# A mixture-of-experts block: the last expert's down matrix by column halves

## The reference, cut to what matters

```python
def expert(args):
    xt, w1e, w3e, w2e = args
    return (jax.nn.silu(xt @ w1e) * (xt @ w3e)) @ w2e

ye = lax.map(expert, (xe.swapaxes(0, 1), w1, w3, w2))
ye = ye.swapaxes(0, 1) * gate[..., None].astype(ye.dtype)
ye = ye.reshape(B, N_EXPERTS * cap, D)
return jax.vmap(lambda y, i: jnp.zeros((S, D), y.dtype).at[i].add(y))(
    ye, idx.reshape(B, N_EXPERTS * cap))
```

## Time and profile before

| | us |
|---|---|
| median of 3 runs | 1906.71 |
| the three runs | 1904.84, 1906.71, 1906.79 |
| span of the profiled execution | 1904.77 |
| the profiled execution's own time | not given apart from its span |
| TensorE busy (share of the span) | 1745.2 (92%) |
| VectorE busy | 550.8 (29%) |
| ScalarE busy | 224.1 (12%) |
| mean rate of the DMAs over the span | 314 GB/s |

### The profile page before, as it was taken

One profiled execution on the slowest core, in us unless ns is written; L12 is line 12 of the kernel. 1 busy time (PEld: TensorE's weight loads), 2 busy tenths in 40 slices (PEclk: granted clock), 3 DMA queues, 4 the chain that ended last, 5 costly groups with the idle time before them and its releaser, 6 DMA issues.

```text
span 1904.8 us, 20203 instructions
## 1 busy us (share of the span) xinstructions
PE 1745.2 (92%) x8202; PEld 774.4 (41%) x8202; DVE 550.8 (29%) x1479; ACT 224.1 (12%) x439; POOL 56.1 (3%) x61
## 2 busy tenths in 40 slices
PE   9999999999999999998988889898898988989888
PEld 8544575544465433332333323333333333323332
DVE  2343373496552322211212022121221112211111
ACT  2331151002471200000000000000000000000000
POOL 0000001053000000000000000000000000000000
PEclk9999999999999999999999999999999999999999
DMA  7102110261207699999999999999999999999998
GB/s 253 52 5 89 45 45 1 90 178 48 88 2 333 267 408 430 430 431 430 431 430 431 430 431 431 431 430 431 431 430 431 431 431 429 431 429 431 431 427 342
DMA packets 56579, 598.55 MB, mean 314 GB/s; under 512 B 6920, under 2 KB 16264, under 8 KB 30424
## 3 DMA queue, kind: packets, MB, share of 16 engines
q1 hardware_dynamic: 56536, 597.96, 75.1%
HBM read 591.42 MB, written 2.10 MB: 312 GB/s over the span
## 4 chain that ended last, share of the span: by engine, by line
DMA 50%; PE 42%; DVE 6%; ACT 1%; issue 1%; DVEq 0%; SPq 0%; ACTq 0%
DMA arena<-in_w 49%; PE PS L1462 10%; PE PS L2016 9%; PE PS L2068 6%; PE PS L1895 3%; PE PS L1731 3%; DVE arena L1205 2%; PE PS L1650 2%; PE PS L1647 2%; ACT arena L777 1%; PE PS L1636 1%; DVE arena L930 1%; PE PS L2083 1%; PE PS L1974 1%; PE PS L1530 1%
## 5 line engine op out<-in xcount | busy, mean ns | idle before, releaser
L2016 PE MATMUL PS<-arena 128*64 128x512 f32 (+1 forms) x3072 | 623.6, 560 | 102.6 <-DMA arena<-in_w 102.6
L2016 PEld LDWEIGHTS PS<-arena 128*64 128x64 f32 x3072 | 213.3, 137 | 507.1 <-issue 364.5
L2068 PE MATMUL PS<-arena 128*64 128x512 f32 x1408 | 320.6, 594 | 24.6 <-DMA arena<-in_w 12.4
L1462 PE MATMUL PS<-arena 128*128 128x512 f32 (+7 forms) x720 | 258.3, 516 | 0.5 <-DMA arena<-in_w_in 0.5
L2068 PEld LDWEIGHTS PS<-arena 128*64 128x64 f32 x1408 | 117.2, 137 | 218.3 <-issue 171.3
L1462 PEld LDWEIGHTS PS<-arena 128*128 128x128 f32 (+1 forms) x720 | 129.3, 187 | 119.5 <-issue 105.5
L1340 DVE TENSOR_SCALAR_CACHE_REDUCE arena<-PS,arena 128x128 f32<-128x128 f32 (+2 forms) x160 | 61.2, 428 | 271.2 <-PE PS L1933 271.2
L1431 DVE TENSOR_TENSOR arena<-arena,PS 128x1408 f32<-128x1408 f32 x16 | 25.9, 1621 | 333.8 <-PE PS L2016 333.8
L833 ACT ACTIVATE arena<-PS 128x1408 f32<-128x1408 f32 x16 | 21.5, 1344 | 733.3 <-PE PS L2016 733.3
L1440 DVE COPY arena<-PS 128x512 f32<-128x512 f32 x16 | 11.1, 692 | 326.2 <-PE PS L2068 326.2
L2083 PE MATMUL PS<-arena 64*128 64x512 f32 x256 | 75.6, 625 | 8.7 <-DVE arena L1423 8.0
(11 more groups left out here) (265 smaller groups left out, 1208.5 us busy)
## 6 DMA issues: line engine op xcount, KB each, us to landing
arena<-in_w SPq DMA_DIRECT2D x181, 2816.0 KB, 34.3
arena<-in_w SPq DMA_DIRECT2D x20, 1408.0 KB, 11.6
arena<-in_w_in SPq DMA_DIRECT2D x6, 2048.0 KB, 8.4
arena<-in_w_in SPq DMA_DIRECT2D x8, 1024.0 KB, 6.6
arena<-in_w_out SPq DMA_DIRECT2D x4, 2048.0 KB, 7.9
arena<-arena SPq DMA_DIRECT2D x64, 67.5 KB, 2.5
arena<-in_tab SPq DMA_DIRECT2D x1, 2304.0 KB
arena<-in_x SPq DMA_DIRECT2D x4, 512.0 KB, 6.6
```

The costliest lines, as they stand in the source:

```text
L1462: i = pe.matmul(dst, lhs(k), rhs(k), start=k == 0, stop=k == KD - 1)
L2016: i = pe.matmul(PS[64 * f:64 * f + 64, bank + c0 // 512, 0:w], XE[:, k, :], slot[:, f * FH + c0:f * FH + c0 + w], start=n % KD == 0, stop= ...
L2068: ins = pe.matmul(PS[64 * d:64 * d + 64, 6, :], HT[:, j, 64 * f:64 * f + 64], W2R[:, f, j, d * 512:(d + 1) * 512], start=f == 0 and j == 0 ...
```

## The change

The last expert's w2 is loaded and multiplied by column halves in place of halves of its rows. Pair 8 now is columns 0 to 511 of half h = 0, pair 9 the same columns of h = 1; pairs 10 and 11 are columns 512 to 1023. So the first 512 columns of the result are complete after pair 9, and the other 512 after pair 11.

- **Loads** (`last_rows`, `LAST_ROWS`): each pair is 128 partitions x 11 rows x 512 columns, that is runs of 2 KB out of rows of 4 KB, where it was one run of 22.5 KB for each partition. Pieces: pair 8 whole, 9 and 10 in 6 + 5 rows, 11 in 5 + 4 + 2 rows.
- **Products**: each row j is two matmuls of 256 columns (`LC`) on the two column groups. Column half d goes to bank 6 + d.
- **Copies to YE**: VectorE copies partitions 0 to 63 (columns 0 to 255) twice, to both partition halves of YE, and ScalarE the others twice, so both partition halves of YE hold all 512 columns.
- **Scatter**: 4 matmuls for each column half, alternating between the two partition halves. It stands behind pair 10's products for the first half and behind pair 11's for the second.
- **Preloads**: two for each half, t = 1 and 3; those of the second half wait for ScalarE's copies of the first.
- **Sums and stores**: for each half VectorE adds t = 0 and 2, ScalarE copies t = 1 and 3, SP issues four stores of 256 KB.

One copy and six adds have become two rounds of two copies and two adds. The diff, cut to its core:

```diff
@@ constants
-LAST_CUT = [(11, 0, 2560), (16, 2560, 4608), (20, 4608, 5632)]
-LAST_BANK = [0, 7, 1, 2, 3, 4, 5, 6]
-LAST_ACT = [1, 4]
-LAST_DVE = [0, 2, 3, 5, 6, 7]
+LAST_ROWS = {8: [11], 9: [6, 11], 10: [6, 11], 11: [5, 9, 11]}
+LAST_ACT = [1, 3]
+LAST_DVE = [0, 2]
+LC = 256
@@ SP
+            def last_rows(m, j0, j1):
+
+                rows = w2[E - 1].rearrange("(h p j) d -> h p j d", h=2, p=P)[m % 2]
+                return rows[:, j0:j1, (m - 8) // 2 * 512:(m - 8) // 2 * 512 + 512]
...
+                    if last_one and m >= 8:
+                        for j0, j1, filled in zip([0] + LAST_ROWS[m], LAST_ROWS[m], last_filled(m)):
+                            sp.dma_start(RING[i % PAIRS][:, j0 * 512:j1 * 512].rearrange("p (j c) -> p j c", c=512),
+                                         last_rows(m, j0, j1)).then_inc(filled, 16)
+                        continue
...
-            for t in range(NT):
-
-                sp.wait_ge(s["sc_copy"], sum(n < 2 * t + 2 for n in LAST_ACT))
-                sp.wait_ge(s["sc_add"], (E - 1) * 2 * NT + sum(n < 2 * t + 2 for n in LAST_DVE))
-                sp.dma_start(out[t * P:(t + 1) * P, :], X[:, t, :]).then_inc(s["out_done"], 16)
+            for d in range(2):
+                for t in range(NT):
+                    if t in LAST_ACT:
+                        sp.wait_ge(s["tail_copy"], 2 * d + LAST_ACT.index(t) + 1)
+                    else:
+                        sp.wait_ge(s["tail_add"], 2 * d + LAST_DVE.index(t) + 1)
+                    sp.dma_start(out[t * P:(t + 1) * P, d * 512:(d + 1) * 512], X[:, t, d * 512:(d + 1) * 512]).then_inc(s["out_done"], 16)
@@ ScalarE
+                    for d in range(2):
+                        act.wait_ge(s["ring_used"], e * CHUNKS + 2 * KD + d + 1)
+                        act.activation(YE[64:128, LC:2 * LC], PS[64:128, 6 + d, 0:LC], ACT.Copy)
+                        act.activation(YE[0:64, LC:2 * LC], PS[64:128, 6 + d, 0:LC], ACT.Copy).then_inc(s["ye_act"], 1)
+                        for t in LAST_ACT:
+                            act.wait_ge(s["tail_psum"], NT * d + t + 1)
+                            act.activation(X[:, t, d * 512:(d + 1) * 512], PS[:, t, :], ACT.Copy).then_inc(s["tail_copy"], 1)
@@ VectorE
+                if last_one:
+                    for d in range(2):
+                        dve.wait_ge(s["ring_used"], e * CHUNKS + 2 * KD + d + 1)
+                        if d == 1:
+                            dve.wait_ge(s["tail_psum"], NT)
+                        dve.tensor_copy(YE[0:64, 0:LC], PS[0:64, 6 + d, 0:LC])
+                        dve.tensor_copy(YE[64:128, 0:LC], PS[0:64, 6 + d, 0:LC]).then_inc(s["ye_ready"], 1)
+                        for t in LAST_DVE:
+                            dve.wait_ge(s["tail_psum"], NT * d + t + 1)
+                            xs = X[:, t, d * 512:(d + 1) * 512]
+                            dve.tensor_tensor(xs, xs, PS[:, t, :], ALU.add).then_inc(s["tail_add"], 1)
+                    return
@@ TensorE
+            def last_down(e):
+                def preload(d):
+                    for t in LAST_ACT:
+                        pe.matmul(PS[:, t, :], ident, X[:, t, d * 512:(d + 1) * 512], start=True, stop=False, skip_group_check=True)
+                def products(m, d):
...
+                    for j in range(FJ):
...
+                        for c in range(2):
+                            ins = pe.matmul(PS[64 * c:64 * c + 64, 6 + d, 0:LC], HT[:, j, 64 * (m % 2):64 * (m % 2) + 64],
+                                            slot[:, j * 512 + c * LC:j * 512 + (c + 1) * LC],
+                                            start=m % 2 == 0 and j == 0, stop=m % 2 == 1 and j == FJ - 1, skip_group_check=True)
+                    if m % 2:
+                        ins.then_inc(s["ring_used"], 1)
+                def scatter(d):
+                    pe.wait_ge(s["ye_ready"], e + 1 + d)
+                    pe.wait_ge(s["gates_ready"], e + 1)
+                    pe.wait_ge(s["ye_act"], d + 1)
+                    for t in range(NT):
+                        g = 64 * (t % 2)
+                        pe.matmul(PS[:, t, :], G[g:g + 64, t * P:(t + 1) * P], YE[g:g + 64, :], start=t in LAST_DVE, stop=True,
+                                  skip_group_check=True).then_inc(s["tail_psum"], 1)
+                preload(0)
+                products(8, 0), products(9, 0)
+                products(10, 1)
+                scatter(0)
+                pe.wait_ge(s["tail_copy"], 2)
+                preload(1)
+                products(11, 1)
+                pe.wait_ge(s["tail_add"], 2)
+                scatter(1)
```

More of the change, by code:

```diff
@@ L313, in build @@
         lg_sub lg_exp aff_ready ab_ready abT_psum cnt_done rank_done gates_ready sel_ready aux_ready gx_psum idg_psum idg_ready xt_ready xT_psum xe_ready s1_done hh_done
-        ring_used ht_psum ht_evD ht_evA ye_ready sc_psum sc_add sc_copy out_done act_own dve_own gp_own""".split()
+        ring_used ht_psum ht_evD ht_evA ye_ready sc_psum sc_add ye_act tail_psum tail_add tail_copy out_done act_own dve_own gp_own""".split()
         s = {n: sem(n) for n in names}
@@ L330, in landed, with last_filled @@
             return v * 16 if i % PAIRS == PAIRS - 1 or first and i < PAIRS else v * 16 + 16
+        def last_filled(m):
+            more = tail_in if m == 11 else [half_in[LAST_HALVES.index(m)]] if m in LAST_HALVES else []
+            return [ring_in[place(m, False) % PAIRS]] + more
         ws_level, level = [], [0, 0]
@@ L1436, in expert @@
                 dve.tensor_copy(HT[:, 4:FJ, :], PF[:, 4 * P:FH].rearrange("p (j c) -> p j c", c=P)).then_inc(s["ht_evD"], 1)
-                if not last_one:
-                    gather_out(e + 1, 1)
+                if last_one:
[10 more added lines that the diff above has]
+                    return
+                gather_out(e + 1, 1)
                 dve.wait_ge(s["ring_used"], (e + 1) * CHUNKS)
                 dve.tensor_copy(YE, PS[:, 6, :]).then_inc(s["ye_ready"], 1)
[L1441 to L1444, removed]
+                dve.wait_ge(s["gates_ready"], e + 1)
+                slots_out(e + 1)
+                for n in range(2 * NT):
                     t, d = n // 2, n % 2
@@ L2018, in up13 @@
                     i.then_inc(s["ring_used"], 1)
+            def last_down(e):
[3 more added lines that the diff above has]
+                def products(m, d):
+                    i = place(m, False)
+                    slot = RING[i % PAIRS]
+                    for j in range(FJ):
+                        if j == 0:
+                            pe.wait_ge(ring_in[i % PAIRS], landed(i, 2 * e + 2, False))
+                        elif j in LAST_ROWS[m]:
+                            n = LAST_ROWS[m].index(j)
+                            pe.wait_ge(last_filled(m)[n + 1], 16 if m == 11 else 32)
+                        for c in range(2):
[21 more added lines that the diff above has]
+                scatter(1)
             def expert(e, first, last_one):
@@ L2040, in expert @@
                     gather(e + 1, 1)
[L2041 to L2046, removed]
                 pe.wait_ge(s["hh_done"], e + 1)
@@ L2052, in expert @@
                     gather_turn(e + 1, 1)
-                if last_one:
-                    preload(LAST_ACT[1])
                 pe.wait_ge(s["ht_evA"], e + 1)
                 pe.wait_ge(s["ht_evD"], e + 1)
+                if last_one:
+                    last_down(e)
+                    return
                 for f in range(2):
```

29 lines of the change are left out of this document (7 added, 22 removed).

## The result

The changed kernel is slower. Its median is 1910.99 us (8 runs, 1909.58 to 1911.92), that of the kernel before on the same chip 1906.38. The ratio is 1.0026, with a 95% interval from 1.0017 to 1.0036, that is 3.2 to 6.9 us. The forecast was 1908.4, at most 1911.0, with 0.86 on "within 0.2%". The measured median is inside the 1911.0 by a hair and the difference, 0.26%, is outside the 0.2%: the case that had a chance of 0.10. One more set of runs beside the kernel before gave 1.0023 (1.0013 to 1.0033), with a median of 1910.24.

A forecast was written before the change was run, and what follows sets the result against it. Loads bound the kernel, then the tail behind the last bytes. Last product +4.25 us (pair 10's load +1.25 of it), from there to the last add -2.15, stores -0.4: +1.7 us, 1908.4 on the median, range 1905.5 to 1911.

The forecast's parts named there:

- Part 3: First two preloads, moved behind HT's copies: hold TensorE for 1.72 us, hidden as long as it waits for pair 10.
- rival D: TensorE's clock falls in the tail at waits of 0.6 to 1.0 us; pair 11 costs 4.7 us more, 1913.1; chance 0.03.
- Part 1: Loads of w2, pairs 8 to 11, in 2 KB runs: 403 GB/s instead of 428, pair 10 complete 1.25 us later.
- Part 2: SP's queue: eight loads stay eight, four stores become eight, the first four through by about 1898; costed at nothing.
- Parts 4 and 5: Pair products as 256-column matmuls cost 4.70 us as before; copies of the first half to YE cost nothing.
- Part 6: First scatter, ScalarE's copy and second preloads between pairs 10 and 11: 4.4 us, leaving TensorE 4 us late.
- Part 7: The end: last product to last add shrinks from 5.9 to 3.7 us; stores then end the span at 1906.5.
- Rival A: TensorE keeps up with pair 11, the end follows the last landing: -1.3 us, 1905.4; chance 0.12, faster version 0.04.
- Rival B: 2 KB runs of w2 cost much more, under 367 GB/s; at 350 GB/s +4.9 us, 1911.6; chance 0.07.
- Rival C: A fixed overhead per packet makes the 2 KB runs 4% slower and no more: +1.3 us, 1908.0; chance 0.06.

The follow-up runs named there:

- e1_fill: Changed kernel with one unused-result matmul put back in each of the two gaps where the preloads stood; +2.9 us (1.1 to 4.8) on the kernel before.
- e3_before_2kb: Kernel before with only the last expert's pairs 8 to 11 loaded in 2 KB runs, result wrong; +2.5 us (0.8 to 4.2) on the kernel before.
- e6_one_half: e1_fill without the first half's copies, scatter, sums and two preloads, columns 0 to 511 left out; +0.2 us (-1.5 to +2.1) on the kernel before.
- e7_order: Changed kernel reordered: first preloads in the old gaps, second in banks of their own, first scatter between pairs 9 and 10; -0.2 us (-1.9 to +1.5) on kernel before.
- e4f_fill_long: Changed kernel with both matmuls back in the gaps and the kernel before's long load runs, result wrong; +2.3 us (0.6 to 4.0) on the kernel before.
- e4_after_long: Changed kernel with the kernel before's long load runs for pairs 8 to 11, result wrong; +4.2 us (2.5 to 5.9) on the kernel before.
- e2_before_late_preload: Kernel before with only its two preloads moved behind HT's copies, as the change has them; +2.1 us (0.4 to 3.8) on the kernel before.

## Why the prediction was wrong, point by point

**Part 3, the preloads, failed, and with it rival D.** I found both preloads in time "that TensorE had to wait anyway" and costed their removal from there at nothing. The 1.72 us for four passes was 0.2 short at full clock (1.92 from 1893.71 to the next matmul), and it was 3.3 with the clock down. Rival D named the fall of the clock, but I looked for its gaps where the new waits are, at 1887, 1891 and 1899. The gaps that mattered are the ones that the change widens by taking work out: 0.74 to 1.79 and 0.37 to 1.27 us. Neither stood among my terms, since idle time that gets longer is no cost in a sum. I gave D 0.03. The sign that I had named for it, a granted clock under 0.9 in the tail, is there. Its price of 4.7 us was for pair 11, which ran at full clock. What the fall costs is 1.7 us by the medians. In the profile it is 0.4: there pair 10 ends at 25.0, and with the clock kept at 24.6 (e1_fill).

**Part 1, the load, was undersized.** I took 403 GB/s from stretches of 3 us in two loads and left 389 as a bound; the tail runs at 387. Pair 10's second piece is seen at 22.3 (e1_fill), not 21.5, and pair 10 can't end before 24.6, where I had 23.6. In the changed kernel's profile this is hidden behind the slow clock, in e1_fill it decides, and the kernel before would pay 2.5 us for it (e3_before_2kb).

**Part 2 held.** The tail of the chain has no SP queue in it, the first four stores are through by about 1897.5 (1898 forecast), and the span ends 3.6 us behind the last add, as forecast.

**Parts 4 and 5 held.** 44 passes of 256 columns take 4.97 us; I had 4.97. The first half's copies hold nothing up: the scatter starts right behind pair 10.

**Part 6 held and is the largest cost.** From the end of pair 10 to the start of pair 11 I forecast 4.4 us and it is 4.6: scatter 1.97, copy 0.61, preloads 1.98. Without it the last product ends 3.1 us earlier (e6_one_half).

**Part 7 held.** From the last product to the last add it is 3.7 us, as forecast.

**Rival A** needed the first half's tail to be hidden under the load. It isn't in the given order, and is in e7_order. **Rival B** did not come: it needed under 367 GB/s, the tail has 387, and the load is out of the changed kernel's chain. **Rival C**, a loss of 4% and no more, is out: three pairs took 10% longer (e3_before_2kb).

**The sum.** I forecast +1.7. It is +3.3 in the profile, where pair 10 ends 1.4 later than I had it (1.0 with the clock kept, of which 0.8 is the load, and 0.4 by the clock) and part 6 is 0.2 longer. It is +4.6 in the median. Measured at the last product, the 5.9 us are 4.4 for the order of the work, preloads included (e4f_fill_long), 1.0 for the load (e1_fill less e4f_fill_long) and 0.4 for the clock, and the shorter end gives 2.5 back. The profiled execution is among the two shortest of the eight and has the highest mean clock, 0.998. A fall of 6.8 us as in e4_after_long would fit the others, but no profile of the changed kernel caught one, so the last 1.3 us of the median are explained in part by argument. From +1.7 there were only 2.1 us of room to the 0.2%, and both terms that I had missed or undersized point upward: 0.10 for that side was too little. That the median still lies under my upper bound of 1911.0 is luck: the bound was drawn for a slower load (B), and not for the clock.

## What to carry to other kernels

Ask of every matmul that a change moves out of a wait what the wait is without it. A matmul in a gap can be what keeps TensorE's clock, and its removal then costs more than it ever did itself; the granted clock of that stretch belongs in the list of terms. And work "under the load" is only there if the engine that does it waits for the load at that point: here the scatter with its copies and preloads costs 3 us between pairs 10 and 11 (e6_one_half), and nothing that shows between pairs 9 and 10, with banks of its own for the second preloads (e7_order).

## What the runs showed of the hardware

The granted clock fell in all four profiles of kernels with the gaps of 1.79 and 1.27 us around the transposes: three times inside the second gap (the change twice, e4_after_long), once in the transposes between the two (e2_before_late_preload). It did not fall there in any profile with 0.74 and 1.28, 1.79 and 0.41, or 0.74 and 0.37 to 0.75. It came back while TensorE was busy, after 3.4 us in two profiles and after 6.8 in the two others, so the price of the same two gaps differs, and one profile doesn't tell it. The Trainium skill (TensorE: Matmul & The Clock Gate, "Part 1: The HAM clock gate (the "warmup" mystery)") describes such a gate between 1.2 and 2.4 GHz, set by how busy TensorE has been, and the two levels are those of the rows.

Runs of 2 KB out of rows of 4 KB moved at 386 to 387 GB/s in the tail (1867 to 1889), in all kernels that load all of w2 so, against 416 to 419 for long runs at the same place and 402 to 403 for the same form in loads of in_w_out.
